# Keys of the cross attention turned by VectorE in squares of 32, in another order of chunks

## The reference

```python
    mem_n = rms_norm(mem, norm_mem[l])
    kv = (mem_n @ w_kv_mem).reshape(B, mem_n.shape[1], 2, MEM_HEADS, MEM_HEAD_DIM)
    k, v = kv[:, :, 0], kv[:, :, 1]
    s = jnp.einsum('bqhd,bmhd->bhqm', q, k).astype(jnp.float32) * MEM_HEAD_DIM ** -0.5
...
    u = jax.nn.silu(layer_norm(u, ln_g, ln_b))
```

## Time and profile before

| | us |
|---|---|
| median of 3 runs | 1661.95 (1661.71 to 1662.71) |
| profiled execution, its own time | 1661.48 |
| its span, first to last instruction | 1659.7 |
| TensorE busy | 1648.9 (99%) |
| VectorE busy | 1125.9 (68%) |
| ScalarE busy | 822.5 (50%) |
| mean granted TensorE clock | 0.999 |

### The profile page before, as it was taken

How to read it: one execution, slowest core, us unless ns; L and a number is a source line. 1 busy time by engine, 2 the same in 40 slices (tenths; PEclk the granted TensorE clock), 3 DMA queues, 4 the chain that set the end, 5 groups by cost and what they waited for, 6 DMA issues and landing times.

```text
span 1659.7 us, 23586 instructions
## 1 busy us (share of the span) xinstructions
PE 1648.9 (99%) x7760; PEld 1378.6 (83%) x7760; DVE 1125.9 (68%) x1461; ACT 822.5 (50%) x1050; POOL 102.2 (6%) x154
## 2 busy tenths in 40 slices
PE   9999999999999999999999999999999999999997
PEld 8888888888888888888888888888888888888886
DVE  5678777778986466986568866666666666654453
ACT  7556545555545444556555544444444444344343
POOL 3100100010000000120001200000000000000000
PEclk9999999999999999999999999999999999999999
DMA  7865555556576655564435666666666666565563
GB/s 236 251 204 171 171 165 155 160 160 180 173 219 187 195 203 178 194 196 155 143 128 197 201 192 191 193 197 190 191 190 184 192 202 195 198 215 179 188 214 129
DMA packets 161108, 309.69 MB, mean 187 GB/s; under 512 B 10240, under 2 KB 16896, under 8 KB 160800
## 3 DMA queue, kind: packets, MB, share of 16 engines
q1 hardware_dynamic: 158864, 301.50, 58.9%
q0 software_dynamic: 1488, 6.42, 1.1%
q10 hardware_dynamic: 704, 1.11, 0.2%
HBM read 306.89 MB, written 2.10 MB: 186 GB/s over the span
## 4 chain that ended last, share of the span: by engine, by line
PE 98%; DMA 0%; issue 0%; ACT 0%; DVE 0%; SPq 0%; POOLq 0%; POOL 0%; ACTq 0%; DVEq 0%
PE acc L367 30%; PE acc L369 29%; PE acc L368 29%; PE tp L379 1%; PE acc L584 1%; PE acc L582 1%; PE acc L583 1%; PE sc L494 1%; DMA raw<-in_w_in_dram 0%; PE ov L518 0%; PE sc L499 0%; PE sc L508 0%; PE acc L457 0%; PE acc L459 0%; PE acc L458 0%
## 5 line engine op out<-in xcount | busy, mean ns | idle before, releaser
L1266 DVE TENSOR_TENSOR w_lo<-raw,w_hi 128x1024 fp32r<-128x1024 f32 (+3 forms) x591 | 717.5, 1220 | 415.6 <-ACT w_hi L788 408.3
L788 ACT ACTIVATE w_hi<-raw 128x1024 fp32r<-128x1024 f32 (+3 forms) x591 | 605.5, 1027 | 752.6 <-PE acc L369 721.5
L367 PE MATMUL acc<-w_hi,crossT 128*128 128x512 f32 x832 | 324.8, 390 | 0.1
L368 PE MATMUL acc<-w_lo,crossT 128*128 128x512 f32 x832 | 323.8, 389 | 0.0
L369 PE MATMUL acc<-w_hi,crossT 128*128 128x512 f32 x832 | 323.8, 389 | 0.0
L367 PE MATMUL acc<-w_hi,mixT 128*128 128x512 f32 x732 | 289.6, 396 | 0.4 <-DVE mixT L1284 0.3
L369 PE MATMUL acc<-w_hi,mixT 128*128 128x512 f32 x732 | 285.5, 390 | 0.0
L368 PE MATMUL acc<-w_lo,mixT 128*128 128x512 f32 x732 | 285.1, 389 | 0.0
L367 PEld LDWEIGHTS acc<-w_hi,crossT 128*128 128x128 f32 x832 | 156.2, 188 | 33.1 <-ACTq L1021 0.5
L369 PEld LDWEIGHTS acc<-w_hi,crossT 128*128 128x128 f32 x832 | 156.2, 188 | 32.7
L368 PEld LDWEIGHTS acc<-w_lo,crossT 128*128 128x128 f32 x832 | 156.3, 188 | 31.6
(11 more groups left out here) (268 smaller groups left out, 1548.4 us busy)
## 6 DMA issues: line engine op xcount, KB each, us to landing
raw<-in_w_in_dram SPq DMA_DIRECT2D x104, 512.0 KB, 3.9
raw<-in_w_gate_dram SPq DMA_DIRECT2D x88, 512.0 KB, 4.4
raw<-in_w_up_dram SPq DMA_DIRECT2D x88, 512.0 KB, 3.7
raw<-in_w_down_dram SPq DMA_DIRECT2D x80, 512.0 KB, 4.1
raw<-in_w_kv_mem_dram SPq DMA_DIRECT2D x64, 512.0 KB, 4.4
raw<-in_w_o_dram SPq DMA_DIRECT2D x32, 512.0 KB, 4.3
raw<-in_w_q_mem_dram SPq DMA_DIRECT2D x32, 512.0 KB, 3.6
raw<-in_w_o_mem_dram SPq DMA_DIRECT2D x32, 512.0 KB, 3.7
```

The costliest lines, as they stand in the source:

```text
L367: mm(o, lo, whi, start=first and k == 0, stop=False)
L368: mm(o, hi, wlo, start=False, stop=False)
L788: fn(w_hi[:, s, 0:width], raw[:, s, 0:width], ACT.Copy).then_inc(hi_done, 1)
L1266: V.tensor_tensor(w_lo[:, s, 0:width], raw[:, s, 0:width], w_hi[:, s, 0:width].bitcast(F32), ALU.subtract).then_inc(lo_done, 1)
```

## The change

The memory chunks are taken in the order V V V K K K K V, so chunks 3 to 6 are now keys and 0, 1, 2 and 7 values. TensorE's `turn_stage` and ScalarE's `keys_out` for the keys are gone; instead VectorE turns each key chunk from `stage` into `memKT` in the chunk after (4 to 7), with 16 square transposes spread over the iterations by the list `at` (`key_turn`; in iteration t it does squares `at[t]` to `at[t + 1]`, behind that iteration's `split_lo`). `to_stage` gets the semaphore that it waits on as an argument: at the ends of chunks 4, 5 and 6 it waits for `keys_turned`, since it overwrites the stage that VectorE reads. The layer norm's statistics stay in chunk 4; scaling (now at t = 1 and 2), the turns back and Silu move to chunk 5, the high and low parts of `convT` to chunk 6 (t = 1 and 3). `memV` and `memKT` change places in SBUF. The first pointwise chunk waits for the fourth turn by `keys_turned`.

```diff
-Q_K, Q_D, Q_F, Q_G, Q_H = 15, 19, 23, 24, 28
+Q_D, Q_F, Q_G, Q_H = 15, 19, 20, 24
...
         oT = [sb(middle, f"oT{j}", [P, DK, TOK], F32R) for j in range(2)]
+        memV = sb(middle, "memV", [P, NB, D])
         memKT = sb(middle, "memKT", [P, DK, TOK])
-        memV = sb(middle, "memV", [P, NB, D])
...
-        memv_ready = sem("memv_ready")
+        keys_turned = sem("keys_turned")
...
-            for w_v, n_chunks, n_tiles, first in ((wkv_v, 8, 8, T_E), (wpw_v, 4, 4, T_D), (wo_v, 4, 8, T_F),
+            for n_chunks, col0, first in ((3, D, T_E), (4, 0, T_E + 24)):
+                with sp.Fori(0, n_chunks) as i:
+                    col = sp.snap(i * CH + col0)
+                    for t in range(8):
+                        tile(i * 8 + first, t, wkv_v[:, 2 * t:2 * t + 2, ds(col, CH)], 2, CH)
+            for t in range(8):
+                tile(T_E + 56, t, wkv_v[:, 2 * t:2 * t + 2, D + 3 * CH:2 * D], 2, CH)
+            for w_v, n_chunks, n_tiles, first in ((wpw_v, 4, 4, T_D), (wo_v, 4, 8, T_F),
...
             with pe.Fori(1, 4) as c:
                 for t in range(8):
                     products(c * 8 + T_E, t, 8, *mem_rows(t), 2, CH, c + C_E)
-                    if t == 1:
-                        turn_stage(c + (Q_K - 1), 2 * c + 2 * S_K)
             for t in range(8):
                 products(T_E + 32, t, 8, *mem_rows(t), 2, CH, C_E + 4)
-                if t == 1:
-                    turn_stage(Q_K + 3, 2 * (S_K + 4))
                 if t == 1:
...
@@ -617,6 +620,8 @@
                             ins = turn(banks[j // 4][:, (j % 4) * P:(j % 4 + 1) * P],
                                        conv[:, j, b * P:(b + 1) * P], ident[:, :])
                         ins.then_inc(ln_turned, 1)
+            for t in range(8):
+                products(T_E + 40, t, 8, *mem_rows(t), 2, CH, C_E + 5)
...
+            with pe.Fori(6, 8) as c:
                 for t in range(8):
                     products(c * 8 + T_E, t, 8, *mem_rows(t), 2, CH, c + C_E)
...
-            def to_stage(chunk, last_tile, fills, before, norm):
-                act.wait_ge(turned, before)
+            def to_stage(chunk, last_tile, fills, read, before, norm):
+                act.wait_ge(read, before)
                 for b in range(NB):
...
-            def keys_out(c, q):
-                for g in range(2):
-                    act.wait_ge(turned, 2 * q + (g + 1))
-                    fn(memKT[:, cols(c * 4 + 2 * g, 2), :].rearrange("p k t -> p (k t)"), tp[:, g, :], ACT.Copy)\
-                        .then_inc(turned_out[g], 1)
...
             for t in range(8):
                 if t == 7:
                     act.wait_ge(r_ready, R_MEM + 1)
-                    to_stage(C_E, T_E + 8, 2 * S_K, 2 * (Q_B + 1), R_MEM)
+                    values_out(0, C_E, T_E + 8)
...
-            with act.Fori(1, 4) as c:
+            with act.Fori(1, 3) as c:
                 for t in range(8):
                     if t == 7:
-                        to_stage(c + C_E, c * 8 + (T_E + 8), 2 * c + 2 * S_K, 2 * c + 2 * Q_K, R_MEM)
+                        values_out(c, c + C_E, c * 8 + (T_E + 8))
                     split_hi(c * 8 + T_E, t + 4)
-                    if t == 1:
-                        keys_out(c - 1, c + (Q_K - 1))
             for t in range(8):
                 if t == 7:
-                    values_out(0, C_E + 4, T_E + 40)
+                    to_stage(C_E + 3, T_E + 32, 2 * S_K, turned, 2 * (Q_B + 1), R_MEM)
+                split_hi(T_E + 24, t + 4)
+            for t in range(8):
+                if t == 7:
+                    to_stage(C_E + 4, T_E + 40, 2 * S_K + 2, keys_turned, 1, R_MEM)
                 split_hi(T_E + 32, t + 4)
-                if t == 1:
-                    keys_out(3, Q_K + 3)
+            for t in range(8):
+                if t == 7:
+                    to_stage(C_E + 5, T_E + 48, 2 * S_K + 4, keys_turned, 2, R_MEM)
+                split_hi(T_E + 40, t + 4)
                 if t == 3:
                     load_table(ACT.Silu)
                 if t == 5:
...
+            for t in range(8):
                 if t == 7:
-                    for g in range(2):
-                        act.wait_ge(silu_ready, 4 * g + 4)
-                        fn(convT[0][:, 4 * g:4 * g + 4, :], conv[:, 4 * g:4 * g + 4, :], ACT.Copy)\
-                            .then_inc(convT_hi, 1)
-            with act.Fori(5, 8) as c:
-                for t in range(8):
-                    if t == 7:
-                        values_out(c - 4, c + C_E, c * 8 + (T_E + 8))
-                    split_hi(c * 8 + T_E, t + 4)
+                    to_stage(C_E + 6, T_E + 56, 2 * S_K + 6, keys_turned, 3, R_MEM)
+                split_hi(T_E + 48, t + 4)
+                if t in (1, 3):
+                    g = t // 2
+                    act.wait_ge(silu_ready, 4 * g + 4)
+                    fn(convT[0][:, 4 * g:4 * g + 4, :], conv[:, 4 * g:4 * g + 4, :], ACT.Copy).then_inc(convT_hi, 1)
+            for t in range(8):
+                if t == 7:
+                    values_out(3, C_E + 7, T_E + 64)
+                split_hi(T_E + 56, t + 4)
...
-            def square_turns(t, dst):
-                for n in range((0, 3, 6, 9, 12, 14, 16, 16)[t], (3, 6, 9, 12, 14, 16, 16, 16)[t]):
+            def square_turns(t, dst, at=(0, 3, 6, 9, 12, 14, 16, 16, 16)):
+                for n in range(at[t], at[t + 1]):
...
+            def key_turn(t, c, at=(0, 3, 6, 9, 12, 14, 16, 16, 16)):
+                if t == 0:
+                    dve.wait_ge(stage_full, 2 * c + (2 * S_K + 2))
+                if at[t + 1] > at[t]:
+                    ins = square_turns(t, memKT[:, c * 4:c * 4 + 4, :], at)
+                    if at[t + 1] == 16:
+                        ins.then_inc(keys_turned, 1)
...
-                if t == 2:
-                    dve.wait_ge(r_ready, R_LN + 1)
-                    for b in range(NB):
-                        for h in range(2):
-                            V.tensor_scalar(ln_tok[:, b, h * CH:(h + 1) * CH], banks[b][h], bn2[:, b, 0:1],
-                                            rfac[:, R_LN, b:b + 1], ALU.subtract, ALU.mult).then_inc(ln_ready, 1)
-                if t == 7:
-                    for g in range(2):
-                        dve.wait_ge(convT_hi, g + 1)
-                        V.tensor_tensor(convT[1][:, 4 * g:4 * g + 4, :], conv[:, 4 * g:4 * g + 4, :],
-                                        convT[0][:, 4 * g:4 * g + 4, :].bitcast(F32), ALU.subtract)\
-                            .then_inc(convT_lo, 1)
-            with dve.Fori(5, 8) as c:
-                for t in range(8):
-                    split_lo(c * 8 + T_E, t + 4)
-            def bias_added(b, c, chunk, last_tile, free):
-                dve.wait_ge(turned, free)
+                key_turn(t, 0, (0, 3, 3, 5, 8, 11, 14, 16, 16))
+            for t in range(8):
+                split_lo(T_E + 40, t + 4)
+                if t in (1, 2):
+                    if t == 1:
+                        dve.wait_ge(r_ready, R_LN + 1)
+                    b = t - 1
+                    for h in range(2):
+                        V.tensor_scalar(ln_tok[:, b, h * CH:(h + 1) * CH], banks[b][h], bn2[:, b, 0:1],
+                                        rfac[:, R_LN, b:b + 1], ALU.subtract, ALU.mult).then_inc(ln_ready, 1)
+                key_turn(t, 1, (0, 3, 3, 3, 6, 9, 12, 16, 16))
+            for t in range(8):
+                split_lo(T_E + 48, t + 4)
+                if t in (1, 3):
+                    g = t // 2
+                    dve.wait_ge(convT_hi, g + 1)
+                    V.tensor_tensor(convT[1][:, 4 * g:4 * g + 4, :], conv[:, 4 * g:4 * g + 4, :],
+                                    convT[0][:, 4 * g:4 * g + 4, :].bitcast(F32), ALU.subtract).then_inc(convT_lo, 1)
+                key_turn(t, 2, (0, 3, 4, 7, 8, 11, 14, 16, 16))
+            for t in range(8):
+                split_lo(T_E + 56, t + 4)
+                key_turn(t, 3)
...
-            pointwise(0, True, 2 * (Q_K + 4))
+            pointwise(0, True, keys_turned, 4)
```

More of the change, by code:

```diff
@@ L628, in _ @@
                         ins.then_inc(ln_back, 1)
-            with pe.Fori(5, 8) as c:
+            with pe.Fori(6, 8) as c:
                 for t in range(8):
@@ L1172, in _ @@
                     act.wait_ge(r_ready, R_CROSS + 1)
-                    to_stage(C_G, T_G + 8, 2 * S_G, 2 * (Q_F + 1), R_CROSS)
+                    to_stage(C_G, T_G + 8, 2 * S_G, turned, 2 * (Q_F + 1), R_CROSS)
                 split_hi(T_G, t + 4)
@@ L1180, in _ @@
                     if t == 7:
-                        to_stage(c + C_G, c * 8 + (T_G + 8), 2 * c + 2 * S_G, 2 * c + 2 * Q_G, R_CROSS)
+                        to_stage(c + C_G, c * 8 + (T_G + 8), 2 * c + 2 * S_G, turned, 2 * c + 2 * Q_G, R_CROSS)
                     split_hi(c * 8 + T_G, t + 4)
@@ L1550, in bias_added @@
+            def bias_added(b, c, chunk, last_tile, read, free):
+                dve.wait_ge(read, free)
```

(10 more changed lines are left out.)

## The result

The changed kernel takes 1665.54 us (median of 20 runs, 1663.95 to 1667.35), the kernel before 1662.52 (20 runs, 1661.35 to 1665.19): a ratio of 1.002, with a 95% interval of 1.0014 to 1.0026. It is slower by 3.0 us, a difference near the smallest that can be told from none, and the forecast was 1665.4. In its ten faster executions the mean granted clock is 0.999, in the ten slower ones (from 1665.65 us) 0.998.

The account below looks back on a forecast made before the run. TensorE, busy 99% of the span, was taken as the bound. Terms -3.54 + 5.98 + 1.06 = +3.50 us on the profiled 1661.48 give 1664.98, about 1665.4 in the median; range 1662.9 to 1667.0.

Parts of the forecast that it names:

- The turns that go: TensorE's four keys' turns of 8 transposes each leave the memory chunks: -3.54 us.
- The tap wait: TensorE's first layer-norm turn in chunk 4 waits for VectorE's last convolution tap: +1.06 us, bounds 0.8 and 1.3.
- The boundaries: Ends of chunks 4, 5, 6: TensorE idles for the stage copy, which waits for VectorE's squares: 1.64, 2.70, 1.64, sum +5.98 us.
- The low parts in time, SyncE's loads, the other order, the spread norm: Memory chunks: VectorE's remaining list fits, SyncE loads the same tiles, values first and moved layer-norm work cost nothing.
- The clock: Half rate after a boundary wait: nothing in the sum, longest idle about 2.5 us; left to the fourth rival.
- the fourth rival: Waits add up: fallen clock after chunk 5's wait, or late splits holding a tile: 1667 to 1670 us; chance 0.08.
- The tail: Chunk 7 and everything behind it stay as before; no term in the sum.
- The first rival: Squares end in time and the stage copies at the ends of chunks 4 to 6 hide: 1658.4 to 1659.5 us; chance 0.11.
- The second: Rival: the wait for the last tap in chunk 4 doesn't come: 1664.4 us; chance 0.12.
- third: Rival: only some ends of chunks 4 to 6 wait: 1663.8 us, down to 1661; chance 0.07.

Follow-up runs that it names:

- experiment 6: Changed kernel with squares ahead of splits, layer-norm turns and statistics one tile later, chunk 4's last squares earlier (none in t = 6): 1656.88 us.
- experiments 2: Changed kernel with squares ahead of splits in chunks 4 to 6, and layer-norm turns and statistics one tile later in chunk 4: 1658.53 us.
- Experiments 1: Changed kernel with VectorE doing each iteration's squares ahead of its split in chunks 4 to 6: 1658.97 us, ratio 0.9978.
- experiment 5: Changed kernel with two squares instead of four in chunk 5's t = 6, the other two spread over t = 4 and 5: 1664.28 us.
- experiment 7: Changed kernel with the keys' turns back on TensorE and ScalarE, keeping only the chunk order and spread layer norm: 1661.76 us, ratio 0.9996.
- experiment 3: Changed kernel with only the layer-norm turns and statistics one tile later in chunk 4, squares still behind the splits: 1666.17 us.
- experiment 4: Changed kernel with 9 dummy matmuls on TensorE between chunks 5 and 6, results unread: 1665.16 us, ratio 1.0016.

## Why the prediction was right, step by step

The forecast of 1665.4 stands 0.1 us from the median. The mechanism was right, and the closeness is partly luck. The change itself was forecast at +3.5 us and measured at +3.0; the forecast started from 1661.95, a median of 3 runs, where 20 runs give 1662.52, and this covers the half microsecond. And the +3.0 is a sum of which most terms were right and two were left out that nearly cancel: the fallen clock (+1.5 in the profiled execution) and the tail (-1.1).

- **The turns that go**, -3.54: experiment 6 shows -3.50 with nothing else left, and chunks 1 to 3 take 21.86, 21.76 and 21.76.
- **The tap wait**, +1.06: the last tap ended at 504.76, which is 71.73 us behind the start of chunk 1 (71.93 before), and TensorE was idle for 0.96 and restarted for 0.06. The size was right. What was missing is the lesson of experiments 2 and 6: the wait isn't a term of its own, since with it gone VectorE is as late at the chunk's end, and it takes an earlier place of the last squares as well to gain the microsecond.
- **The boundaries**, 1.64, 2.70 and 1.64, each with 0.10 for the restart: measured 1.69, 2.60 and 1.60 without the restarts, which are 0.08, 0.20 and 0.11 more, so 6.28 in place of 5.98. The copies begin 3.5, 4.5 and 3.5 us into tile 7, as forecast. All links held: the split behind ScalarE's high part, squares of 0.436 us on average, 0.04 to ScalarE. Experiments 1 and 5 show that the position of the squares and their number set it. In experiment 1 the copy at 1.89 us hid to within 0.1 us, where the prediction had put the limit at about 1.9.
- **The low parts in time, SyncE's loads, the other order, the spread norm**, each at nothing: no wait of TensorE in chunks 1 to 3, and experiment 7, which tests the order and the norm, is 0.18 us over before in the stage.
- **The clock**, the term that was mis-sized. The text said: "My longest idle is about 2.5 us, shorter than the stretch at full clock in the tail, so the sum takes nothing for it." The idle time was 2.44 us, and the price 1.5 us in the profiled execution. The reading of the earlier trace rows was wrong in that it took the granted clock during the idle time for the answer. Here it is 1.00 in 550 to 551 too, while TensorE waits, and the first matmul after it is spaced as at any restart (0.34 us); the fall comes near 551.4. So the fourth rival, given 0.08, was in part what happened, at 1.5 us rather than the 2.7 of a whole tile, and, as the spread of the times suggests, not in every execution. The Trainium skill (TensorE: Matmul & The Clock Gate, "Part 1: The HAM clock gate") lets an idle array fall to half rate; the trace agrees in the level, 0.50 in 552 to 554, which stands behind the idle time and not in it.
- **The tail**, -1.1, which no step had. Everything behind chunk 7 was forecast "as before", and it was not. The diff doesn't touch that code.

The first rival (hidden turns, 1658.4 to 1659.5) failed for this kernel for the reason it gave against itself, the fixed order of VectorE's queue, and is what experiment 1 makes of it (1658.97). The second and third didn't happen.

## What to carry to other kernels

Where an engine runs its instructions in order, work that releases a hand-over (here a square that frees a buffer) must not stand behind an instruction that is gated by the other engine's progress (here the last split of a chunk), if that one has slack and the first has none: this order cost 6.6 us with the same work in it. An engine's average idle time doesn't tell whether it is late at one moment, so a saving on the bound engine has to be checked at each place where the helping engine must already be done, and a wait removed at one of them may only move to the next. Compare kernels by the lengths of the same stage, since here head and tail shifted by a microsecond and more for reasons elsewhere.

## What the runs showed of the hardware

A wait of TensorE can cost more than its length. Behind 2.44 us of idleness (changed kernel) the granted clock went to 0.50 after the work had begun again, and 8 matmuls took 3.33 us instead of 1.82. Behind 2.45 us (chunk 5 of experiment 3) and 2.09 us in the head (experiment 5) it was already down at the restart. Behind 2.05 us (chunk 4 of experiment 3), 1.54 us (experiment 5) and 1.53 us (chunk 4 of the changed kernel), and with dummy matmuls in the gap (experiment 4), it stayed at 1.00. These are single executions; whether the 2.44 us cost the clock each time isn't shown, and what tells the 2.05 from the 2.09 is open.

With a change of code far ahead the tail of the program was 1.1 us shorter, alike in the changed kernel and its seven variants against two executions of before, and two packets of instruction loads stand in the longer one. The cause was not isolated.
